# Output matrix of the odd layer: the attention rows of three chunks as plain fp32 products among RWKV's inversions

## The reference

```python
def odd_mixer(h, w_in, w_out, ...):
    p = h @ w_in
    q, k, v = jnp.split(p[..., :3 * DSA_QKV], 3, axis=-1)
    ...                                   # three dilated window attentions
    y_c = jnp.sum(wts[..., None] * jnp.stack(outs), axis=0).reshape(B, S, DSA_OUT)
    ...                                   # RWKV-7 scan in both directions
    y_d = (yn + (bonuses[0] + bonuses[1]).reshape(B, S, RW_WIDTH)) * gate
    return jnp.concatenate([y_c.astype(h.dtype), y_d.astype(h.dtype)], axis=-1) @ w_out
```

## Time and profile before

| | |
|---|---|
| device time, three runs | 2760.33, 2761.34, 2762.03 us (median 2761.34) |
| profiled execution, its own time | 2761.37 us |
| its span, first to last instruction | 2759.4 us |
| PE busy | 2721.2 us (99%) |
| DVE busy | 1542.7 us (56%) |
| ACT busy | 1311.5 us (48%) |
| granted TensorE clock, mean | 0.997 of full |
| RWKV's inversions, on the span's clock | 1745.6 to 1875 us |
| `od_out` | 1891.2 to 1935.5 us |

### The profile page before, as it was taken

The page is one execution under the profiler, slowest core; times in us unless marked ns, Lnnn a source line. Parts: engine busy times, 40 slices in busy tenths (PEclk is TensorE's granted clock), DMA queues, the critical chain, the costliest instruction groups (busy, mean ns, idle before and its releaser), DMA issues.

```text
span 2759.4 us, 44057 instructions
## 1 busy us (share of the span) xinstructions
PE 2721.2 (99%) x18158; PEld 2390.1 (87%) x18158; DVE 1542.7 (56%) x2048; ACT 1311.5 (48%) x1798; POOL 119.8 (4%) x167
## 2 busy tenths in 40 slices
PE   8999999999999999999999999999999999999999
PEld 7999998888888888888898997888888888888887
DVE  5655465666555555545544665656665555555554
ACT  4544444556544534445444344334555444354453
POOL 0000043000000000000000000440000000000000
PEclk9999999999999999999999999999999999999999
DMA  7554500543555555555545553004445555555554
GB/s 276 182 183 166 182 34 33 211 170 139 183 200 195 183 198 183 192 189 183 194 172 202 195 208 109 2 2 153 168 152 184 198 183 192 190 185 196 186 194 138
DMA packets 67788, 461.48 MB, mean 167 GB/s; under 512 B 7024, under 2 KB 10224, under 8 KB 13085
## 3 DMA queue, kind: packets, MB, share of 16 engines
q1 hardware_dynamic: 63824, 449.47, 45.5%
q10 hardware_dynamic: 3500, 5.21, 0.6%
q0 software_dynamic: 288, 4.19, 0.4%
HBM read 456.73 MB, written 5.27 MB: 167 GB/s over the span
## 4 chain that ended last, share of the span: by engine, by line
PE 94%; DVE 3%; ACT 2%; issue 1%; DMA 0%; POOL 0%; DVEq 0%; ACTq 0%; POOLq 0%
PE bank L423 17%; PE bank L402 13%; PE bank L404 13%; PE bank L403 13%; PE bank L425 9%; PE bank L446 6%; PE bank L448 6%; PE bank L447 6%; PE bank L1197 1%; PE bank L1170 1%; PE bank L337 1%; PE bank L2475 1%; PE bank L561 0%; PE bank L505 0%; DVE split_lo L353 0%
## 5 line engine op out<-in xcount | busy, mean ns | idle before, releaser
L353 DVE TENSOR_TENSOR split_lo<-raw,split_hi 128x1024 fp32r<-128x1024 f32 x840 | 1019.6, 1224 | 932.8 <-ACT split_hi L346 932.2
L346 ACT ACTIVATE split_hi<-raw 128x1024 fp32r<-128x1024 f32 x840 | 881.5, 1059 | 1127.3 <-PE bank L404 554.9
L423 PE MATMUL bank<-hT,split_hi 128*128 128x512 f32 x2048 | 721.0, 397 | 0.0
L425 PE MATMUL bank<-hT,split_lo 128*128 128x256 f32 x2048 | 574.7, 281 | 0.0
L423 PEld LDWEIGHTS bank<-hT,split_hi 128*128 128x128 f32 x2048 | 384.4, 188 | 92.8
L402 PE MATMUL bank<-split_hi,u_hi 128*128 128x512 f32 x1152 | 449.7, 390 | 0.0
L404 PE MATMUL bank<-split_hi,u_lo 128*128 128x512 f32 x1152 | 448.4, 389 | 0.0
L403 PE MATMUL bank<-split_lo,u_hi 128*128 128x512 f32 x1152 | 448.4, 389 | 0.0
L425 PEld LDWEIGHTS bank<-hT,split_lo 128*128 128x128 f32 x2048 | 386.9, 189 | 0.2
L446 PE MATMUL bank<-hT,split_hi 128*128 128x256 f32 x1328 | 376.8, 284 | 0.0
L447 PE MATMUL bank<-hT,split_hi 128*128 128x256 f32 x1328 | 375.8, 283 | 0.0
(11 more groups left out here) (469 smaller groups left out, 2260.3 us busy)
## 6 DMA issues: line engine op xcount, KB each, us to landing
raw<-in_stream SPq DMA_DIRECT2D x420, 1024.0 KB, 4.8
work<-in_mem POOLq DMA_DIRECT2D x2, 2048.0 KB, 9.0
bias_rows<-bias_line SPq DMA_DIRECT2D x1, 3072.0 KB, 13.3
x<-in_x SPq DMA_DIRECT2D x1, 2048.0 KB, 9.1
out<-x SPq DMA_DIRECT2D x4, 512.0 KB, 5.0
mwork<-bias_rows ACTq DMA_DIRECT2D x1, 1536.0 KB, 10.0
work<-bias_rows ACTq DMA_DIRECT2D x1, 1536.0 KB, 9.8
rwork<-in_wide ACTq DMA_DIRECT2D x1, 1280.0 KB, 6.1
```

What stands on the lines that cost most here:

```text
L346: nc.scalar.activation(split_hi[:, u % SPLIT], raw[:, b % RAW, (u % 2) * UNIT:(u % 2 + 1) * UNIT], ACT.Copy).then_inc(s_hi, 1)
L353: nc.vector.tensor_tensor(split_lo[:, u % SPLIT], raw[:, b % RAW, (u % 2) * UNIT:(u % 2 + 1) * UNIT], f32(split_hi[:, u % SPLIT]), SUB).th ...
L423: nc.tensor.matmul(out[:, :], lhsT=w_hi[:, cols], rhs=hT[:, k].rearrange("p two s -> p (two s)"), start=k == 0, stop=False)
L425: m = nc.tensor.matmul(out[:, S:2 * S], lhsT=w_lo[:, cols], rhs=hT_hi[:, k, :], start=False, stop=k == KD - 1)
```

## The change

A new entry `od_early` of the stream (no chunk, six units) holds the attention rows (512) of columns 512 to 2047, that is of chunks 1 to 3 of `od_out`. It stands ahead of `od_out`, whose chunks 1 to 3 keep only the RWKV rows (2 units instead of 4, k = 4 to 7). The six early units are not split. `pe_early` multiplies them straight from `raw` with the fp32 `ycT` (attention's output, stored in the memory of `mem_kT`), for chunk c and token tile t four products of 128x512, k = 0 to 3, into one bank; `dve_early` adds that bank to x. The 24 products stand where `pe_fill` stood, and in four more slots of f = 3; the six additions stand in DVE's order. New waits see to it that the banks are free. The order of the weight stream in DRAM follows. In both MLPs the turning of the last two batches moves from k = 6 to k = 8.

```diff
-    ("od_q", 3, 8), ("od_k", 3, 8), ("od_rw", 4, 8), ("od_v", 3, 8), ("od_out", 4, 4),
+    ("od_q", 3, 8), ("od_k", 3, 8), ("od_rw", 4, 8), ("od_v", 3, 8), ("od_early", 0, ()), ("od_out", 4, (4, 2, 2, 2)),
...
+EARLY = {"od_early": 6}
...
             out.row_chunk(0, tile_of, k_tiles=k_tiles, k_ready=k_ready, after_unit=after_unit)
-            out.row_chunk(1, tile_of, k_tiles=k_tiles)
-            out.row_chunk(2, tile_of, k_tiles=k_tiles)
-            out.row_chunk(3, tile_of, k_tiles=k_tiles)
+            for c in range(1, 4):
+                out.row_chunk(c, lambda k, t: tile_of(k + early, t), k_tiles=k_tiles - early)
...
-                    if turn == 0 and k == 6:
+                    if turn == 0 and k == 8:
...
-            pe_fill(bank[4], 12)
+            pe.wait_ge(s_rgs, 1)
+            pe_early(pe, 1, 0, range(4))
             pe_rwkv_pairs(pe, 0, 0)
             pe.wait_ge(s_rgs, 2)
+            pe.wait_ge(s_early_x, 1)
             pe_rwkv_pairs(pe, 0, 1)
             pe.wait_ge(s_rMAT, 1)
-            pe_fill(bank[0], 16)
+            pe_early(pe, 1, 1, range(4))
             for f in range(RW_F):
                 def between(slot):
                     if f == 0 and slot in (3, 7):
-                        pe_fill(bank[0], 7 if slot == 3 else 10)
-                    if slot == 20 or (f and slot == 23):
+                        pe.wait_ge(s_rMAT, 4)
+                        pe_early(pe, 2, 0, range(2) if slot == 3 else range(2, 4))
+                    if f in (1, 2) and slot in (20, 23):
+                        pe_early(pe, f + 1, 2 - f, range(2) if slot == 20 else range(2, 4))
+                    elif slot == 20 or (f and slot == 23):
                         pe_fill(bank[0], 4 if slot == 20 else 7)
+                    if f == RW_F - 1 and slot in (2, 3, 5, 6):
+                        pe.wait_ge(s_rMAT, 8 * RW_F)
+                        pe_early(pe, 3, 1, ((2, 3, 5, 6).index(slot),))
...
+            pe.wait_ge(s_early_x, 6)
             pe_out_cross(pe, 1, "od_out", 8, hT_tile, lambda k: pe.wait_ge(s_yT, 9 + k // 2),
-                         lambda u: turn_heads(1) if u == 1 else None)
+                         lambda u: turn_heads(1) if u == 1 else None, early=XA_H)
...
+        def early_bank(c, t):
+            return bank[{(1, 0): 2, (1, 1): 0, (2, 0): 1, (2, 1): 0, (3, 0): 0, (3, 1): 2}[c, t]]
+        def pe_early(pe, c, t, tiles):
+            first = starts["od_early"][1] + 2 * (c - 1)
+            b = first // 2
+            for k in tiles:
+                if (t, k) == (0, 0):
+                    pe.wait_ge(s_raw[b % RAW], (b // RAW + 1) * 16)
+                m = nc.tensor.matmul(early_bank(c, t)[:, :], lhsT=ycT[:, k, t * P:(t + 1) * P],
+                                     rhs=raw[:, b % RAW, k * 512:(k + 1) * 512], start=k == 0, stop=k == XA_H - 1)
...
+        def dve_early(dve, c, t):
...
+            cols = x[:, t, c * 512:(c + 1) * 512]
+            nc.vector.tensor_tensor(cols, cols, early_bank(c, t)[:, :], ADD).then_inc(s_early_x, 1)
...
 def pe_rwkv_tail(pe, f, step):                      # step 0
+                pe.wait_ge(s_early_x, 3 + min(f, 2))
...
 def dve_rwkv(dve):
             dve_rwkv_scales(dve, 0)
+            dve_early(dve, 1, 0)
...
+                    if f == 0 and slot in (2, 6):
+                        dve_early(dve, *((1, 1) if slot == 2 else (2, 0)))
+                    if f == RW_F - 1 and slot == 6:
+                        dve_early(dve, 3, 1)
...
+                    if f in (1, 2) and slot == 11:
+                        dve_early(dve, f + 1, 2 - f)
```

More of the change, by code:

```diff
@@ L87, with units_before @@
     ("mem_k0", 1, 8), ("xa_q0", 1, 8), ("mem_v0", 1, 8), ("xa_o0", 4, 2), ("ffn0", FF_TURNS * FF_CHUNKS, 8),
-    ("od_q", 3, 8), ("od_k", 3, 8), ("od_rw", 4, 8), ("od_v", 3, 8), ("od_out", 4, 4),
+    ("od_q", 3, 8), ("od_k", 3, 8), ("od_rw", 4, 8), ("od_v", 3, 8), ("od_early", 0, ()), ("od_out", 4, (4, 2, 2, 2)),
     ("mem_k1", 1, 8), ("xa_q1", 1, 8), ("mem_v1", 1, 8), ("xa_o1", 4, 2), ("ffn1", FF_TURNS * FF_CHUNKS, 8),
 ]
-UNITS_OF = {name: units for name, _, units in GEMMS}
+UNITS_OF = {name: units if isinstance(units, tuple) else (units,) * chunks for name, chunks, units in GEMMS}
+EARLY = {"od_early": 6}
+def units_before(name, c):
+    return sum(UNITS_OF[name][:c])
 def gemm_starts():
     at, chunk, unit = {}, 0, 0
-    for name, chunks, units in GEMMS:
+    for name, chunks, _ in GEMMS:
         at[name] = (chunk, unit)
         chunk += chunks
-        unit += chunks * units
+        unit += sum(UNITS_OF[name]) + EARLY.get(name, 0)
     return at, chunk, unit
@@ L278, in build @@
         s_rows = sem("s_rows")
+        s_early, s_early_x = sem("s_early"), sem("s_early_x")
         s_ok, s_okt, s_okT_a, s_okT_d = (
@@ L356, in build @@
         next_hi, next_lo = [0], [0]
+        early_units = {starts[name][1] + i for name, count in EARLY.items() for i in range(count)}
         def hi_upto(act, n):
             while next_hi[0] < min(n, n_units):
-                write_hi(act, next_hi[0])
+                if next_hi[0] not in early_units:
+                    write_hi(act, next_hi[0])
                 next_hi[0] += 1
@@ L364, in lo_upto @@
             while next_lo[0] < min(n, n_units):
-                write_lo(dve, next_lo[0])
+                if next_lo[0] not in early_units:
+                    write_lo(dve, next_lo[0])
                 next_lo[0] += 1
@@ L374, in __init__ @@
                 self.chunk0, self.unit0 = starts[name]
-                self.per = UNITS_OF[name]
+                self.name = name
             def unit(self, n):
@@ L396, in row_chunk @@
                     if k % 2 == 0:
-                        w_hi, w_lo = self.unit(c * self.per + k // 2)
+                        w_hi, w_lo = self.unit(units_before(self.name, c) + k // 2)
                     cols = slice((k % 2) * 512, (k % 2 + 1) * 512)
@@ L416, in wide_chunk @@
                     for j in range(2):
-                        w_hi, w_lo = self.unit(c * self.per + 2 * i + j)
+                        w_hi, w_lo = self.unit(units_before(self.name, c) + 2 * i + j)
                         for kk in range(8):
@@ L433, in column_chunk @@
                     for j in range(2):
-                        n = c * self.per + 2 * i + j
+                        n = units_before(self.name, c) + 2 * i + j
                         w_hi, w_lo = self.unit(n)
@@ L457, in chunk_done @@
         def chunk_done(name, c):
-            return starts[name][1] + UNITS_OF[name] * (c + 1)
+            return starts[name][1] + units_before(name, c + 1)
         def chunk_banks(name, c):
@@ L708, in build, with pe_out_cross @@
         xpT = W(12288, NT, XA_H, S)
-        def pe_out_cross(pe, l, out_name, k_tiles, tile_of, k_ready, after_unit):
+        def pe_out_cross(pe, l, out_name, k_tiles, tile_of, k_ready, after_unit, early=0):
             out = Gemm(pe, out_name)
             out.row_chunk(0, tile_of, k_tiles=k_tiles, k_ready=k_ready, after_unit=after_unit)
-            out.row_chunk(1, tile_of, k_tiles=k_tiles)
-            out.row_chunk(2, tile_of, k_tiles=k_tiles)
-            out.row_chunk(3, tile_of, k_tiles=k_tiles)
+            for c in range(1, 4):
+                out.row_chunk(c, lambda k, t: tile_of(k + early, t), k_tiles=k_tiles - early)
             if l == 0:
@@ L2427, in pe_rwkv @@
             turn_heads(0)
+            pe.wait_ge(s_early_x, 6)
             pe_out_cross(pe, 1, "od_out", 8, hT_tile, lambda k: pe.wait_ge(s_yT, 9 + k // 2),
-                         lambda u: turn_heads(1) if u == 1 else None)
+                         lambda u: turn_heads(1) if u == 1 else None, early=XA_H)
[9 more added lines that the diff above has]
+                                     rhs=raw[:, b % RAW, k * 512:(k + 1) * 512], start=k == 0, stop=k == XA_H - 1)
+                if (t, k) == (0, 0):
+                    m.then_inc(s_used, 2)
+                elif (t, k) == (0, 1):
+                    m.then_inc(s_hi, 2)
+                elif (t, k) == (0, XA_H - 1):
+                    m.then_inc(s_early, 1)
+                elif (t, k) == (1, XA_H - 1):
+                    m.then_inc(s_lo, 2)
+        def dve_early(dve, c, t):
+            if t == 0:
+                dve.wait_ge(s_early, c)
+            else:
+                dve.wait_ge(s_lo, starts["od_early"][1] + 2 * c)
+            cols = x[:, t, c * 512:(c + 1) * 512]
+            nc.vector.tensor_tensor(cols, cols, early_bank(c, t)[:, :], ADD).then_inc(s_early_x, 1)
         RW_PE = {'tail': (0, 1, 4, 8, 9, 10), 'cum': 0, 'pairs': (15, 21)}
@@ L2444, in pe_rwkv_bonus @@
             pe.wait_ge(s_rMAT, 4)
+            pe.wait_ge(s_early_x, 2)
             for t in range(NT):
@@ L3032 @@
             got = column_units(matrices[name])
+        elif name in EARLY:
+            late, rows = "od_out", 512
+            got = np.concatenate([row_units(matrices[late][:rows, c * 512:(c + 1) * 512]) for c in range(1, 4)])
```

(2 more changed lines are left out.)

## The result

| kernel | median, us | from, to, us | executions | ratio to before, 95% interval |
|---|---|---|---|---|
| before | 2761.16 | 2758.58 to 2763.87 | 13 | |
| after | 2769.24 | 2760.41 to 2771.23 | 13 | 1.0023 [1.0014, 1.0032] |

The change makes the kernel slower by 0.23%, 8 us; 2756.6 was predicted. The 13 executions of the changed kernel fall into two groups: three at 2760.41 to 2761.95 us with a mean granted clock of 0.997, and ten at 2767.99 to 2771.23 with 0.993 or 0.994. The profiled one took 2769.39 us (span 2767.6, clock 0.994) and belongs to the ten.

A forecast was written before the change was run, and what follows sets the result against it. PE was taken to bound the kernel, busy 99% of the span; -16.3 + 1.3 + 6.0 + 3.6 + 0.6 + 0.8 - 0.8 = -4.8 us from 2761.37 gave 2756.6 us, range 2750 to 2764.

The forecast's parts named there:

- the clock in the new stalls: Rival: half clock at the new PE stalls, 3.4 us each; chance 0.25 for one or both, 0.05 for more stretches.
- The sum: All terms of the prediction without a fall of the clock: -4.8 us, giving 2756.6 us; chance 0.4.
- The stalls: From f = 1 to 2 and f = 2 to 3, tail's step 0 waits for DVE's addition: 3.0 us later each, +6.0.
- The rival that they don't: Rival: PE's hidden slack in f = 2 and f = 3 makes both boundaries cost 0.7 each, giving 2752.0 us; chance 0.25.
- `od_out`: Chunks 1 to 3 lose k = 0 to 3, 72 products of 0.227 us: -16.3 us, the whole gain.
- the +0.8: Behind RWKV, splits and halvings on ACT make PE wait 0.9 us for turned x instead of 0.4: 0 to 2.
- The move to k = 8: Turning later lets PE pass over two waits of 1.3 us together: 0 to -1.3, taken as -0.8.
- f = 0: Later inversion start and two more additions in DVE's order: 0.64 to 1.92 us, taken as +1.3.
- f = 3: Four early products replacing no unread ones, +3.6 us, and one addition in level 4 of the inversion, +0.6.
- ACT as the bound of `od_out`: Rival: nothing is gained in `od_out`, a wait of 5 us in place of 0.9, giving 2761; chance 0.05.

The follow-up runs named there:

- experiment 4: The changed kernel once more, unedited, on the same chip as later runs: 2767.17 us, ratio 1.0023; its profile is of the lower group.
- experiment 5: Changed kernel with DVE's early addition moved ahead of the inversion's first step at f = 1 alone, 2758.23 us, or f = 2 alone, 2759.00 us.
- both of 6: Changed kernel with the last two batches turned at k = 6 again, 2760.57 us; the same plus six unread products ahead of RWKV, 2765.03 us.
- experiment 3: Kernel before, with only an added wait: the tail's step 0 waits for a DVE multiplication by 1 at the end of f = 1 and 2; 2771.54 us.
- experiment 7: Kernel before with the last two batches of x turned at k = 8 in both MLPs and nothing else: 2762.34 us, ratio 1.0003.
- experiment 1: Changed kernel with DVE's early addition ahead of the next inversion's first step at the end of f = 1 and f = 2: 2754.19 us, ratio 0.9975.
- experiment 2: Changed kernel with nine unread products on PE ahead of the wait of the tail's step 0 in f = 1 and f = 2: 2759.88 us, ratio 0.9997.

## Why the prediction was wrong

**The step that failed is the clock in the new stalls.** The sum puts it at nothing; as the first rival it had 0.25 for one or both, 0.05 for more, at 3.4 us each. By the runs it was the likeliest case, and its price was too narrow. In the changed kernel's profile the first boundary lost 3.4 us and the second 6.8; in four other profiles with the same first wait (experiments 4, 5 and both of 6) the first lost 1.7, and in three of these the second lost nothing. The sum without clock and the measured clock give -4.8 + 10.4 = +5.6; +8.2 was measured between the two spans, of which 1.5 lie ahead of f = 0, in that execution, and 1.0 behind the first addition of `od_out`.

The argument against the rival was that large products stand right ahead of each stall. They do (L2466 at 1813.94), and the clock fell all the same. The price came from the earlier trace rows, both from stretches with other work behind them; behind the second wait, the half clock lasted for more than 12 us in which PE's records show no gap. Nothing in the rows of before bounded that from above, so the range should have reached further than two times 3.4.

The Trainium skill ("TensorE: Matmul & The Clock Gate", section "Why this matters for your kernels") warns of long idle gaps between bursts. By it, as the prediction said, neither stall would have mattered. The runs here disagree: the clock fell behind waits of 2.28 us, and in experiment 3 behind waits of 2.1 us, though not in every execution.

**The terms**, by steps of the prediction:

- *The stalls:* 2.28 us each, 2.2 foreseen (2.3 by the prediction's own times), at the place and by the releaser named. They reach the end of the stage: in experiment 4's profile step 0 to step 0 takes 38.7 us in f = 2 (1817.65 to 1856.32) and 33.7 before; less the 1.8 of clock that is +3.2, where 3.0 was foreseen. The rival that they don't is out.
- *`od_out`:* the additions of chunks 0 to 2 are 5.44 us apart, as foreseen, and PE goes on at that pace through chunk 3. The wait for the turned x is 1.77 where 0.9 was foreseen, so the +0.8 was +1.4.
- *The move to k = 8:* foreseen at -0.8. The two waits of together 1.3 us are gone from the profile, but experiment 7 shows no gain and does not exclude one. With +1.4 and nothing for the move the part behind the first addition should be -16.3 + 1.4 = -14.9; it measured -15.3.
- *f = 0:* it starts 0.6 us later than the products ahead of it explain (1747.71 - 1731.91 against 1745.58 - 1730.38) and is 0.8 longer to the start of f = 1 (1747.71 to 1779.95, 1745.58 to 1777.05 before): +1.4, foreseen 1.3. In experiment 4's profile it is +0.9.
- *f = 3:* +4.4 at full clock, foreseen 4.2.
- *ACT as the bound of `od_out`:* no; PE goes through the four chunks without a wait for a split.

**What stays open:** what decides, from one execution to the next, whether the clock falls behind the second wait. By the times it did in 14 of 19 executions of the changed kernel (counting those at 2766 us and above) and in 5 of 12 with the first boundary mended. The waits are of one length in both kinds (2.28 and 2.29 us in the two profiles of the changed kernel). Open too is why the clock falls at the end of f = 3 in some profiles and not in others, with or without the waits.

## What to carry to other kernels

In this kernel the unread products that kept PE busy also kept its clock: whoever puts useful work with a result in their place adds a consumer, and the first thing to ask is where on that consumer's engine the addition stands, and what PE does until it ends. After these runs, a stall of 2 us on PE in such a stage is to be priced at its own length plus a stretch at half clock that can be several times as long, with a range that has both; it should be the likely case until a profile shows otherwise. Here one line of order on DVE was worth more than the whole change: look for the operation that frees a bank and put it ahead of what waits for other engines.

## What the runs showed of the hardware

- One wait of 2.3 us, in the same kernel, cost about its length in some executions and about 10 us more in others (experiment 5: medians of 2756.2 and 2766.0 us, beside 2754.2 in experiment 1); the kernel that keeps only the first such wait had one group, within 3.6 us, and lost 1.7 us of clock behind it in its profile.
- The half clock can last while PE's records show no gap: 1860 to 1872, PE busy for 4.00 of 4 us in each stretch at 0.50, with 64-wide products and two-record groups of 128x512. A product that takes 1.13 us there otherwise took 2.07.
- Products that nobody reads kept the clock at 1.00 through a stall of 2.3 us (experiment 2), at no cost that could be seen beside the stall's own.
- A wait is not needed for a fall: in the kernel before the clock was 0.59 in the mean of 1776 to 1784, where PE's records fill 8.00 of 8 us.
